# The rounded half of the weight tiles of the recurrent heads, made by ScalarE instead of GpSimd

## The reference

```
z = u @ w_in
aq, ak, av, ag, hq, hf_f, hf_b, hv, hg = jnp.split(z, SPLIT_IDX, axis=-1)
...
f = lb + (1.0 - lb) * jax.nn.sigmoid(f_logit)
...
    b = jnp.cumsum(gc, axis=2)
    diff = b[:, :, :, None, :] - b[:, :, None, :, :]
    decay = jnp.exp(jnp.where(tri[:, :, None], diff, -jnp.inf))
    att = jnp.einsum('bhtk,bhsk,bhtsk->bhts', qc, kc, decay)
```

## Time and profile before

| what | us |
|---|---|
| median of 3 runs (lowest, highest) | 3165.94 (3164.91, 3169.05) |
| the profiled execution | 3168.32 |
| its span in the trace | 3167.0 |
| PE busy in the span | 3012.2 (95%) |
| POOL busy | 1971.5 (62%) |
| DVE busy | 1772.1 (56%) |
| ACT busy | 1007.3 (32%) |

### The profile page before, as it was taken

The page is one execution under the profiler, slowest core; times in us unless marked ns, Lnnn a source line. Parts: engine busy times, 40 slices in busy tenths (PEclk is TensorE's granted clock), DMA queues, the critical chain, the costliest instruction groups (busy, mean ns, idle before and its releaser), DMA issues.

```text
span 3167.0 us, 39581 instructions
## 1 busy us (share of the span) xinstructions
PE 3012.2 (95%) x15184; PEld 2359.0 (74%) x15184; DVE 1772.1 (56%) x2397; ACT 1007.3 (32%) x1720; POOL 1971.5 (62%) x1860
## 2 busy tenths in 40 slices
PE   7999999999999999999998999999899999799997
PEld 5787777788778878777876777776677777588686
DVE  5754897751484569777128433335678888500512
ACT  5333223330233331333012322224444444311422
POOL 5566576577676667756768565554566676277363
PEclk9999999999999999999999999999999999899998
DMA  5222222233223322222422222222122222232122
GB/s 205 87 107 101 82 98 87 80 138 121 107 93 110 111 77 98 85 87 87 178 98 95 84 69 83 76 75 72 56 79 78 70 81 73 106 108 93 66 91 83
DMA packets 60876, 298.67 MB, mean 94 GB/s; under 512 B 6512, under 2 KB 7408, under 8 KB 31248
## 3 DMA queue, kind: packets, MB, share of 16 engines
q1 hardware_dynamic: 38496, 251.67, 22.9%
q10 hardware_dynamic: 22192, 44.48, 4.1%
HBM read 274.04 MB, written 16.84 MB: 92 GB/s over the span
## 4 chain that ended last, share of the span: by engine, by line
PE 75%; DVE 16%; ACT 5%; issue 2%; POOL 1%; ACTq 1%; DMA 0%; DVEq 0%; POOLq 0%
PE bank L423 65%; DVE h_lo L1809 1%; PE bank L765 1%; DVE rec_ex L2408 1%; DVE norm_y L1848 1%; PE bank L782 1%; PE bank L774 1%; POOL w_lo L2574 1%; ACT att_sc L1310 1%; PE bank L858 1%; DVE rec_lk L2421 1%; DVE rec_cum L2380 1%; DVE rec_lq L2419 1%; DVE bank L1880 1%; PE bank L833 1%
## 5 line engine op out<-in xcount | busy, mean ns | idle before, releaser
L423 PE MATMUL bank<-h_hi,w_lo 128*128 128x512 f32 x3712 | 1507.6, 406 | 46.9 <-POOL w_lo L2574 19.5
L423 PE MATMUL bank<-h_hi,w_hi 128*128 128x512 f32 x3712 | 1458.7, 393 | 0.0
L423 PE MATMUL bank<-h_lo,w_hi 128*128 128x512 f32 x3712 | 1457.1, 393 | 0.0
L2572 POOL TENSOR_SCALAR w_hi<-w_raw 128x512 fp32r<-128x512 f32 x928 | 698.3, 752 | 1080.4 <-PE bank L423 1000.3
L2574 POOL TENSOR_TENSOR w_lo<-w_raw,w_hi 128x512 fp32r<-128x512 f32 x928 | 1295.8, 1396 | 77.5
L423 PEld LDWEIGHTS bank<-h_hi,w_lo 128*128 128x128 f32 x3712 | 703.3, 189 | 260.3 <-issue 50.8
L423 PEld LDWEIGHTS bank<-h_hi,w_hi 128*128 128x128 f32 x3712 | 702.9, 189 | 152.2
L423 PEld LDWEIGHTS bank<-h_lo,w_hi 128*128 128x128 f32 x3712 | 704.3, 190 | 147.5 <-issue 10.6
L1022 ACT ACTIVATE raw<-bank 128x512 f32<-128x512 f32 x148 | 88.5, 598 | 397.6 <-PE bank L423 360.0
L2079 DVE SCALAR_TENSOR_TENSOR bank<-cfm_up,par,bank 128x512 f32<-128x512 f32 x232 | 175.4, 756 | 8.3
L1795 DVE TENSOR_TENSOR sumsq<-sumsq,bank 128x512 f32<-128x512 f32 x80 | 55.0, 687 | 184.5 <-ACT bank L1708 150.1
(11 more groups left out here) (364 smaller groups left out, 2747.0 us busy)
## 6 DMA issues: line engine op xcount, KB each, us to landing
w_raw<-in_wall SPq DMA_DIRECT2D x230, 1024.0 KB, 4.9
x_scratch<-xT ACTq DMA_DIRECT2D x12, 1024.0 KB, 5.4
xT<-x_scratch ACTq DMA_DIRECT2D x12, 1024.0 KB, 8.1
ssd_abc<-acs_scratch ACTq DMA_DIRECT2D x16, 512.0 KB, 3.8
first_xin<-in_x SPq DMA_DIRECT2D x4, 1024.0 KB, 11.0
out<-last_z SPq DMA_DIRECT2D x4, 1024.0 KB, 4.1
w_raw<-in_wall SPq DMA_DIRECT2D x8, 256.0 KB, 9.9
att_tq<-att_uq ACTq DMA_DIRECT2D x32, 64.0 KB
```

Of the source, the lines that this page charges most:

```text
L423: mm = t.matmul(bank[BANK[u]][:, :], w[:, CS16[k]], h[:, k, :], start=(k == 0 and w is m.w_lo[b]), stop=(k == KT - 1 and w is m.w_hi[b] an ...
L2572: g.tensor_scalar(m.w_hi[b][:, part], m.w_raw[b][:, part], 1.0, 1.0, ALU.mult, ALU.mult).then_inc(*s.hi.inc(u, n))
```

## The change

A set `BY_ACT` names 34 units: those two places behind hf, hb, hq and hv of heads 1 to 7 and behind hg of heads 0 to 5. They are the units 166 to 199 and feed the heads 1 to 7. For these, ACT makes the whole rounded half in one operation of 128x2048 right behind the evacuation of unit u-2, after waiting for the load. POOL makes only the four rests, and waits for ACT's operation first. All other units stay as they were.

```diff
+BY_ACT = frozenset(u + 2 for (n, l, j), u in UNIT.items()
+                   if (n in ("hf", "hb", "hq", "hv") and j) or (n == "hg" and j < 6))
...
     def evac(name, dst):
...
         a.activation(dst, bank[BANK[u]][:, :], ACT.Copy).then_inc(*act.inc("evac", u))
+        if u + 2 in BY_ACT:
+            b = u % 2
+            a.wait_ge(*s.raw[b].at(u + 2))
+            a.activation(m.w_hi[b][:, :], m.w_raw[b][:, :], ACT.Copy).then_inc(*act.inc("w_hi", u + 2))
...
     def split(u, n):
         b, part = u % 2, slice(n * PIECE, (n + 1) * PIECE)
-        g.tensor_scalar(m.w_hi[b][:, part], m.w_raw[b][:, part], 1.0, 1.0, ALU.mult, ALU.mult).then_inc(*s.hi.inc(u, n))
-        g.wait_ge(*s.hi.at(u, n))
+        if u in BY_ACT:
+            g.wait_ge(*s.act.at("w_hi", u))
+        else:
+            g.tensor_scalar(m.w_hi[b][:, part], m.w_raw[b][:, part], 1.0, 1.0, ALU.mult, ALU.mult).then_inc(*s.hi.inc(u, n))
+            g.wait_ge(*s.hi.at(u, n))
         g.tensor_tensor(m.w_lo[b][:, part], m.w_raw[b][:, part], m.w_hi[b][:, part].bitcast(F32), ALU.subtract).then_inc(
             *s.lo.inc(u, n))
```

## The result

| what | before | with the change |
|---|---|---|
| median of 4 runs each (us) | 3167.19 | 3194.15 |
| lowest, highest | 3164.91, 3169.05 | 3192.59, 3195.10 |
| ratio, 95% interval | | 1.0083 [1.0071, 1.0096] |
| span of the profiled execution | 3167.0 | 3192.3 |
| POOL busy | 1971.5 | 1847.8 |

The change makes the kernel slower by 27 us (22 to 30 by the interval). The forecast was +14.5 us and a range up to 3191: the sign and the mechanism at levels 2 and 4 were right, the size was little more than half, and the time lies outside the range.

A forecast was written before the change was run, and what follows sets the result against it. PE, busy 95%, was taken as the bound, with waits at small levels for the ACT-DVE-PE chain. Heads 1 to 6 +18.5, head 0 0, head 7 -4 gave +14.5 us: median 3180, range 3166 to 3191.

The forecast's parts named there:

- the chain at level 4: Copy, exponentials, then DVE products alternating with subtractions: level 4 ready 6.8 us after u1's evacuation ends (t), 2.4 later than before.
- no harm from the other 20 copies: Copies behind u2, u3 and u4 in heads 1 to 6 delay nothing PE waits for: 0 us.
- Rival 3: Not slower: DVE, relieved of POOL's interference, wins at levels 4 to 6; -16 us, 3150, chance 0.10.
- head at full clock: Each of heads 1 to 6 without low clock: +1.2 at level 2, +2.4 at level 4, -1.4 at levels 6 and 7.
- low clock, net: One 3.4 us low-clock stretch in each of heads 1 to 6, costing 1.6 us, less the last 0.1 of wait.
- six heads: Heads 1 to 6 together take 445.2 us against 426.7: +18.5.
- up to head 0, and head 0: Head 0, no part of PE's idle time clearly going or growing: estimated 0.
- head 7 to the end: Head 7: POOL silent from near blocks to first exponentials, ten DVE operations 0.6 faster each: -4 us (-5.5 to -2).
- The old 1.5 us of waits there shrink to 0.1: Levels 6 and 7: level 6 ready at t+16.0, PE arriving at t+16.2, so PE's waits nearly vanish.
- rival 2: Two low-clock stretches in each of heads 1 to 6, another 6 x 1.6: +24 us, 3190, chance 0.15.
- Rival 1: The clock falls no more often than now: +9.5 for heads 1 to 6, -4 for head 7, +5.5, 3171; chance 0.20.
- 0, between one relief of 2 and one delay of 2: Head 0: unit 166's split leaves DVE's far chain (gain); copies delay levels 1 and 4, logs 1.9 later (loss).

The follow-up runs named there:

- the kernel with held subtractions: The changed kernel, but in heads 1 to 6 POOL starts the rests of u2 and u3 only after DVE's products of levels 2 and 4: 3170.65 us, ratio 1.0007.
- the later-place kernel: The changed kernel with all 34 copies on ACT, but those of u0 and u1 behind the exponentials of levels 2, 3 and 4, 5: 3153.95 us, ratio 0.9955.
- the kernel with 17 fillers: The changed kernel plus 17 idle identity matmuls on PE ahead of level 4 in heads 1 to 6: 3190.72 us, ratio 1.0097.

## Why the prediction was right and wrong

**Right:** the copies (1.905 us each for 1.92), the chain at level 4 (t+6.8, wait 4.1: measured t+6.8 and 4.07), level 2 (1.2: 1.16), products of 1.6 to 1.7 (1.75 and 1.63), no harm from the other 20 copies, and little change ahead of the recurrent heads (1.3 us in the profiled executions). That levels 6 and 7 don't wait came true too, but by luck: slow matmuls, and not an early level 6, hid the waits. Rival 3 was rightly put low for this place of the copies; its reason against ("back to back for over 5 us, right where those products lie") is what the kernel with held subtractions shows. Beside the copy at 2494.14 in the later-place kernel the differences took 2.27, no more than anywhere, while products beside subtractions took up to 1.9 in place of 0.69. The Trainium skill's rule (SBUF — State Buffer, Who interferes with whom), that DVE and GpSimd share a port pair that one of them locks while ScalarE has its own ports, agrees with these rows. As a reason for the change it counted only once the copies stood behind the exponentials.

**Wrong, by the steps of the sum** (forecast +14.5, measured +25.3 in the profiled spans):

| step | forecast | measured | off by |
|---|---|---|---|
| head at full clock | 72.7 | 73.8 | +1.1 a head |
| low clock, net | +1.5 | +1.3 | -0.2 a head |
| six heads | +18.5 | +24.0 | +5.5 |
| up to head 0, and head 0 | 0 | -3.1 + 7.1 | +4.0 |
| head 7 to the end | -4 | -2.6 | +1.4 |

*Levels 6 and 7.* The step that failed most is "The old 1.5 us of waits there shrink to 0.1". I let the exponentials of level 6 start at t+9.1; they start at t+9.95 (2449.60 against t = 2439.65). The difference pair ahead of them takes 2.27 where nothing meets it (the later-place kernel) and 3.17 here, because the last subtraction, stretched by the turns, runs until 2447.5. The forecast left 2.3 for it, the undisturbed time. That 0.9 is passed on undiminished, since the products of level 6 stand behind the gate in DVE's list and the gate behind the exponentials and the sigmoids in ACT's. At full clock these waits would be 1.1 to 1.4, not 0.1, as the kernel with 17 fillers shows. That is the +1.1 a head, 6.6 of the 10.8 us by which the sum was short; the clock below takes 1.2 back.

*The clock.* The forecast counted one stretch of 3.4 us a head at 1.6; the heads had 6.8 us, as rival 2 had it. But a slow stretch costs its whole price only where no wait lies behind it. Here 1.1 of 2.4 us merely took the place of the waits at levels 6 and 7, and the net is 1.3. So the forecast of one stretch was wrong, and its price for six heads nearly right, by two errors that cancel: luck. The rows of the kernel before could have told me. Its heads 2 and 6 had the clock low for 3.4 us right behind level 4, and took 70.3 us, no longer than heads 4 and 5 at full clock (70.5), since they had no waits at levels 6 and 7. Its heads 1 and 3, with the stretch behind these waits, took 72.3 and 72.7. Head 2, then its stretch at the low clock:

```profile
2327.60:2397.90 70.30, 68.62 (x495) 54.24 (x494) 54.69 (x57) 30.64 (x51) 47.74 (x41) 0.98 0.23 76
2362.50:2365.90 3.40, 3.40 (x9) 2.68 (x9) 3.23 (x3) 1.51 (x3) 3.32 (x3) 0.50 0.02 5
```

So the price of 1.6 each was wrong for two of the four stretches. Rival 1 has another slip: it says that the clock falls as often as now, but its +9.5 for the six heads (6 x 72.7 less 426.7) leaves out every low stretch; with those of the kernel before kept it is 6 x 2.2 = +13.2, and 3175 in place of 3171. The measured 7.6 us are 0.24% of the kernel and all the same a third of what the change costs. The Trainium skill (TensorE: Matmul & The Clock Gate, The HAM clock gate) puts the penalty of warming up at under 1% of a typical kernel; the 0.24% agrees with that.

*Head 0.* "0, between one relief of 2 and one delay of 2" held for the relief (1.9 at the far blocks) and failed for the delay. I had no row that clearly grew, and took that for zero, when level 4 there has the same chain as in the other heads, and level 1 a tighter one: levels follow each other with less work of PE between them. DVE in head 0 with the change, the differences ahead of level 1's products, then these:

```profile
2198.61 3.32 DVE L2414 TENSOR_TENSOR rec_ex<-rec_cum 128x512 f32<-128x512 f32 x2
2202.06 1.55 DVE L2425 TENSOR_TENSOR rec_lq<-rec_ex,rec_qs 128x512 f32<-128x512 f32 x1
2203.64 1.63 DVE L2427 TENSOR_TENSOR rec_lk<-rec_ex,rec_kd 128x512 f32<-128x512 f32 x1
```

Four operations of DVE behind the copy meet four subtractions, and PE waits 5.11 instead of 1.41. The step that was right for heads 1 to 6 was not applied there. Of the 3.1 us by which head 0 starts earlier, 1.9 are the shorter wait (3.90 to 2.03); the other 1.3 were there before the first moved operation.

*Head 7.* Level 0 waits 3.0 instead of 5.78, a relief of 2.8, but level 1, which waited for nothing, now waits 2.8, and starts no earlier behind the far blocks than before. From there to the combination 1.8 us are gained: levels 2, 3 and 5 wait 1.98, 2.71 and 0.07 in place of 3.40, 0.10 and 1.91, and the clock is low for 10.2 us in place of 17. The last 0.8 of the 2.6 lie behind the combination, where the edit changes nothing. So the -2.6 is inside the bound (-5.5 to -2), but its way is not the forecast one, and no run takes it apart.

The bounds came from the same terms as the sum, and the terms for levels 6 and 7, head 0 and head 7 all missed on the same side. In the first two the forecast left out a delay that the operations behind the moved copy had, beyond the copy's own.

## What to carry to other kernels

An operation moved to an idle engine costs by its place in that engine's list: look for the latest place from which its reader is still in time, behind whatever starts a chain that PE waits for. Here moving 14 copies behind the exponentials turned 0.8% slower into 0.3 to 0.5% faster. Where the moved operation also releases work on a third engine, its place is that engine's start signal too, so lay out what will then run beside what, for every level and not only for the one with the longest wait. And price a low clock against the waits behind it: it costs only what they can't swallow.

## What the runs showed of the hardware

- A product of DVE of 0.69 us takes 1.6 to 1.9 when it meets a subtraction of POOL, and POOL's take longer too (5.9 us for four, against 1.3 each). At level 4 a start 10 ns ahead of POOL's rounding goes with a wait of 0.55, a start at the same time with 1.68.
- With the change the granted clock was 1.2 GHz for 6.8 us at each of the seven waits of 4.07 us; with PE filled there, never in heads 1 to 6. With only u1's copy moved, the same wait brought 6.8 us in three heads and 3.4 in the other three. At waits of 2.06 us it fell in three heads of six, for 3.4 us. What makes the difference between equal waits stays open.
- In the kernel before, 3.4 us at 1.2 GHz ahead of the waits at levels 6 and 7 cost nothing (heads of 70.3 against 70.5), and behind them about 2 us (72.3 and 72.7).
- A pair of differences at level 6 takes 2.27 us undisturbed, against 1.42 for the coarser pairs of the same 128x512: the same operation with a finer pattern of access is slower (that it is the pattern wasn't tried by itself).
- A float32 matmul of 128x128 on the identity took 0.228 us, one behind the other.
